# Decode rows of a Mamba-2 mixer turned into columns by four TensorE transposes instead of four fp32 matmuls on identity columns

## The chip, the cores and the metric

One NeuronCore of a Trainium2 chip runs the whole kernel. The metric is the device time of one execution in microseconds (us); lower is better. The kernel works on five engines, each with its own instruction stream: TensorE (PE in the profile, with PEld for its weight loads), VectorE (DVE), ScalarE (ACT), GpSimd (POOL) and SyncE (SP), which issues most DMAs. They meet only through semaphores.

## The reference, cut to what matters

The program is one inference step of a two-layer decoder for two request groups that share the weights: a prompt of 256 tokens and eight decode sequences of one token each (so 264 columns in all). Layer 0 has a Mamba-2 mixer. What the change touches is the decode side of its state-space step, which for one token is

```python
def step(h, inp):                      # T = 1 for the decode sequences
    s_c, dec_c = inp                   # dt * x * B^T, exp(dt * a)
    return h * dec_c[..., None, None] + s_c, h
...
y_inter = jnp.einsum('bclgn,bcgepn->bclgep', cc, h_in) * jnp.exp(cum)[..., None]
y = (y_intra + y_inter)
```

With one token that is y = exp(dt a) (C . h0) + dt (C . B) x. There are 8 groups g, each with 4 heads of 64 values (256 rows of output per sequence) and a state width of 128.

## The kernel before, in words

Everything is kept with channels on the 128 partitions and the 264 tokens along the free axis. Weights come in units of 1024 columns into a ring of four buffers; ScalarE rounds a unit to its high part (`whi`, L985), VectorE computes the rest (`wlo`, L1407), and TensorE makes three products for each tile (L436, L437, L438), 24 products for a unit of the mixer's input projection.

The mixer's input projection ("sin") has 49 units. Its loop runs over slots `s_`, on every engine in the same order: slot `s_` starts with unit `s_`, and other work is put between units by tables: `CHUNK_AT = [14, 17, 21, 25, 30, 35, 41, 46]` (the prompt's scan, two chunks of 128 tokens for each group: `chunk_in(2g)` in that slot, `chunk_in(2g+1)` and `chunk_out(2g)` one later, `chunk_out(2g+1)` two later), `DEC_AT = [16, 19, 23, 27, 32, 37, 43, 46]` (the decode rows) and `NORM_AT`. The order is written out by hand; no planner moves anything. VectorE takes the finished unit out of its bank (`take`, L1454) at the start of its own slot and lags TensorE by up to some microseconds; the semaphores decide by how much.

The decode path of a group g runs so:

- `decode_rows(g)`, TensorE, slot `DEC_AT[g]` (L799): eight matmuls whose stationary operand is C of one sequence, broadcast over 32 columns, put C . h0 into bank 7: 128 rows by 512, where 32 rows in a row hold the same numbers (sequence q mod 4 by row, q div 4 by half of the bank).
- `copy_rows(g)`, ScalarE, same slot (L1188): bank 7 into `crow` in SBUF.
- `decode_columns(g)`, TensorE, slot `DEC_AT[g] + 1` (L814, L816): the 256 rows are wanted as channels on partitions. Four fp32 matmuls with a 128x128 slice of `crow` as stationary operand and four columns of the identity (`ident[:, 0:P:32]`) as moving operand write 16 columns into bank 2; a fifth matmul with `ones` adds the sum over the state of B C, 8 columns. An fp32 matmul appears in the profile as two passes, so L814 has 8 records for each group.
- `decode_read(g)`, VectorE, slot `DEC_AT[g] + 2`, after `take` (L1718, L1720): two small products out of bank 2. GpSimd adds the parts up (L2068, L2069).

Bank 7 is used for one more thing: the differences of the odd chunks, written by `chunk_in(2g+1)` (`diff = bank[5 + 2 * c]`, L759 and L760) and read by ScalarE's `decay_exp(2g+1)` (L1181). Its users before wait on `dec_copied` (the copy to `crow` is done) and on `ssd_exp` (the exponential is done).

Of the kernel before, what the change touches and what calls it, by code (L numbers as in the profile page):

```python
# [19 lines left out]
ALU = mybir.AluOpType  # L20
AX = mybir.AxisListType

P = 128
# [3 lines left out]
SEQS = 8  # L27
N = T + SEQS
# [4 lines left out]
G = 8  # L33
# [61 lines left out]
CHUNK_AT = [14, 17, 21, 25, 30, 35, 41, 46]  # L95
# [3 lines left out]
DEC_AT = [16, 19, 23, 27, 32, 37, 43, 46]  # L99
# [17 lines left out]
def h0_turn(g):  # L117

    return H0_BUF[:g + 1].count(H0_BUF[g])
# [30 lines left out]
def trunk_kernel(nc, weights, xT, pT, cst, vec, convst, ssm0, kcT, vc_in, ck, cv,  # L150
# [3 lines left out]
    with ExitStack() as ctx:  # L154
        def sb(name, shape, dt=F32):
            return ctx.enter_context(nc.sbuf_tensor(name, shape, dt))

        def sem(name):
            return ctx.enter_context(nc.semaphore(name))
# [9 lines left out]
        with nc.sbuf_tensor("under", [P, 2 * FT * N], F32) as under:  # L169
# [4 lines left out]
            crow = under[:, 40 * N + 256:40 * N + 768]  # L174
# [20 lines left out]
        bank = [ctx.enter_context(nc.psum_tensor(f"bank{b}", [P, 512], F32)) for b in range(4)]  # L195
# [5 lines left out]
        ident, tri, ones = cs[:, C_ID:C_ID + P], cs[:, C_TRI:C_TRI + P], cs[:, C_ONE:C_ONE + P]  # L201
# [49 lines left out]
        dec_copied = sem("dec_copied")  # L251
        dec_sel = sem("dec_sel")
        dec_read = sem("dec_read")
# [10 lines left out]
        ssd_exp = sem("ssd_exp")  # L264
# [78 lines left out]
        da_d = sb("da_d", [P, XT, SEQS])  # L343
        dt_d = sb("dt_d", [P, XT, SEQS])
        dtx_d = sb("dtx_d", [P, G, SEQS, 2])
        bc_d = sb("bc_d", [P, G, SEQS])
# [26 lines left out]
        w1 = [guf[:, 576 + 16 * b:592 + 16 * b].rearrange("p (k s) -> p k s", k=2) for b in range(2)]  # L373
        w2 = [guf[:, 608 + 16 * b:624 + 16 * b].rearrange("p (k s) -> p k s", k=2) for b in range(2)]
# [55 lines left out]
        def _(pe):  # L430
            pe.sem_inc(unit_used, RING)

            def split_products(out, w, tile, rh, rl, start, stop):

                c = slice(tile * P, tile * P + P)
                pe.matmul(out, whi[:, w, c], rh, start=start, stop=False)  # L436
                pe.matmul(out, whi[:, w, c], rl, start=False, stop=False)  # L437
                return pe.matmul(out, wlo[:, w, c], rh, start=False, stop=stop)  # L438
# [233 lines left out]
            def sout_part(j, tiles, last=False):  # L672

                pe.wait_ge(lo_ready, U0["sout"] + j + 1)
                pe.wait_ge(hl_ready, HREADY["sout"] + j + 1)
                for m in tiles:
                    mm = split_products(bank[m][:, 0:N], (U0["sout"] + j) % RING, m, hh[:, j, :], hl[:, j, :], j == 0, False)
                if last:
                    mm.then_inc(unit_used, 1)
# [59 lines left out]
            def chunk_in(k):  # L739

                g, c = k // 2, k % 2
                r = slice(128 * c, 128 * c + 128)
                if c == 0:
                    pe.wait_ge(conv_act, 4 * g + 4)
                if k > 0:
                    pe.wait_ge(ssd_read, k)
                pe.matmul(bank[4][:, 0:128], xact[:, 16 + g, r], xact[:, 24 + g, r], start=True, stop=True)
                pe.transpose(bank[4][:, 128:256], xact[:, 16 + g, r], ident)
                pe.transpose(bank[4][:, 256:384], xact[:, 2 * g, r], ident)
                pe.transpose(bank[4][:, 384:512], xact[:, 2 * g + 1, r], ident).then_inc(ssd_in, 1)  # L750
                pe.wait_ge(ssd_sel, k + 1)
                if k > 1:
                    pe.wait_ge(ssd_exp, k - 1)
                if c == 1:
                    pe.wait_ge(dec_copied, [d_ < CHUNK_AT[g] + 1 for d_ in DEC_AT].count(True))
                if k == 0:
                    pe.wait_ge(pre_const, 1)
                diff = bank[5 + 2 * c][:, 0:512]
                pe.matmul(diff, diffLg[k % 2], diffR[c], start=True, stop=False)  # L759
                pe.matmul(diff, ident_r, mask_r.unsqueeze(1).to_broadcast([P, 4, P]), start=False, stop=True).then_inc(ssd_diff, 1)  # L760
# [22 lines left out]
            def add_inter(g):  # L783

                pe.wait_ge(ssd_isc, g + 1)
                for n_ in range(2):
                    mm = pe.matmul(bank[6][:, 256 * n_ + 128:256 * n_ + 256], isc[:, 128 * n_:128 * n_ + 128], ident,
                                   start=False, stop=True, skip_group_check=True)
                mm.then_inc(ssd_tr, 1)

            def decode_rows(g):

                pe.wait_ge(h0_landed[H0_BUF[g]], 16 * h0_turn(g))
                pe.wait_ge(dec_act, g + 1)
                pe.wait_ge(ssd_exp, 2 * [c_ + 1 < DEC_AT[g] for c_ in CHUNK_AT].count(True))
                if g > 0:
                    pe.wait_ge(dec_copied, g)
                for q in range(SEQS):
                    mm = pe.matmul(bank[7][32 * (q % 4):32 * (q % 4) + 32, 256 * (q // 4):256 * (q // 4) + 256],  # L799
                                   dact[:, g, 1, q:q + 1].to_broadcast([P, 32]), h0buf[H0_BUF[g]][:, 256 * q:256 * q + 256], start=True, stop=True)  # L800
                mm.then_inc(h0_used, 1)

            def decode_columns(g):

                pe.wait_ge(dec_copied, g + 1)
                pe.wait_ge(dec_prod, g + 1)
                if g > 0:
                    pe.wait_ge(dec_read, g)
                if DEC_AT[g] + 1 > NORM_AT[3]:
                    pe.wait_ge(gated_std, 1)  # L810
                c_ = N + 24 * g
                for i in range(2):
                    for t in range(2):
                        pe.matmul(bank[2][:, c_ + 8 * t + 4 * i:c_ + 8 * t + 4 * i + 4], crow[:, 256 * i + 128 * t:256 * i + 128 * t + 128],  # L814
                                  ident[:, 0:P:32], start=True, stop=True)
                pe.matmul(bank[2][:, c_ + 16:c_ + 24], ones, bc_d[:, g, :], start=True, stop=True).then_inc(dec_sel, 1)  # L816

            def norm_sums(g):

# [54 lines left out]
            for s_ in range(len(SIN)):  # L874
                if s_ == 1:
                    unit_pair("sin", 0)
                elif s_ > 1:
                    sin_unit(s_)
                if s_ == PRE_AT:
                    pre_tokens()  # L880
                if s_ == PRE_AT + 3:
                    pre_sums()
                for g in range(G):
                    if s_ == CHUNK_AT[g] + 3:
                        add_inter(g)
                if s_ in DEC_AT:
                    decode_rows(DEC_AT.index(s_))
                for g in range(G):
                    if s_ == CHUNK_AT[g]:
                        chunk_in(2 * g)  # L890
                    if s_ == CHUNK_AT[g] + 1:
                        chunk_in(2 * g + 1)
                        chunk_out(2 * g)
                    if s_ == CHUNK_AT[g] + 2:
                        chunk_out(2 * g + 1)
                if s_ in NORM_AT:
                    norm_sums(NORM_AT.index(s_))
                if s_ - 1 in DEC_AT:
                    decode_columns(DEC_AT.index(s_ - 1))
            pe.wait_ge(ssd_read, 2 * G)  # L900
            pe.wait_ge(ssd_exp, 2 * G)
            sout_part(0, (4, 5, 7))
            add_inter(G - 1)
            pe.wait_ge(a_free, A0["f2i0"] + 4)
# [496 lines left out]
        def _(dve):  # L1401
# [308 lines left out]
            def decode_read(g):  # L1710

                dve.wait_ge(dec_sel, g + 1)
                if g == 0:
                    dve.wait_ge(pre_a, 3)
                if g >= 2:
                    dve.wait_ge(dec_y, g - 1)
                c_ = N + 24 * g
                dve.tensor_tensor(w1[g % 2], bank[2][:, c_ + 16:c_ + 24].unsqueeze(1).to_broadcast([P, 2, SEQS]),  # L1718
                                  dtx_d[:, g].rearrange("p s t -> p t s"), ALU.mult)
                dve.tensor_tensor(w2[g % 2], bank[2][:, c_:c_ + 16].rearrange("p (k s) -> p k s", k=2), da_d[:, 2 * g:2 * g + 2, :], ALU.mult).then_inc(dec_read, 1)  # L1720

            def by_head(a):
                return a.rearrange("p (h w) -> p h w", h=4)
# [66 lines left out]
            for s_ in range(SLOTS):  # L1790
                kind, i = SIN[s_] if s_ < len(SIN) else ("", 0)
# [9 lines left out]
                if s_ - 2 in DEC_AT:  # L1801
                    decode_read(DEC_AT.index(s_ - 2))
# [537 lines left out]
```

## Time and profile before

| | before |
|---|---|
| median of 3 runs | 1229.14 us (1228.28 to 1231.04) |
| profiled execution, first to last instruction (span) | 1227.6 us |
| TensorE busy | 1202.2 us, 98% |
| VectorE, ScalarE, GpSimd busy | 882.4, 686.4, 232.8 us |
| chain that ended last, share by engine | PE 69%, DVE 16%, ACT 7%, issue 6%, DMA 2% |
| granted TensorE clock, mean | 0.994 |

For the profiled execution only the span is given, no total of its own; the median of the runs shown is 1.5 us above it. A busy TensorE is not a TensorE at its peak: the matmuls are pipelined, a record of 0.28 us follows the one before it after 0.12 us. The distance between starts is therefore what an instruction costs TensorE.

### The profile page before, as it was taken

What the parts mean: (1) busy time and instruction counts of PE and PEld (TensorE: products, weight loads), DVE (VectorE), ACT (ScalarE), POOL (GpSimd) and SP (SyncE); (2) the same over time, 40 slices, a digit from 0 to 9 for tenths busy, and PEclk for the clock granted to TensorE, in tenths of its full rate; (3) what the DMA queues carried; (4) which work ended last, traced back from release to release, by engine and by line L of the source; (5) the groups of instructions that cost most, each with busy time, mean ns of one, the idle gap of its engine ahead of it and who ended that gap; (6) DMA issues with size and microseconds to landing.
All of it is one profiled execution on the core that took longest, in us unless ns stands there. A gap on an engine that the chain in (4) does not pass through costs nothing.

```text
span 1227.6 us, 26707 instructions
## 1 busy us (share of the span) xinstructions
PE 1202.2 (98%) x9875; PEld 1169.6 (95%) x9875; DVE 882.4 (72%) x1405; ACT 686.4 (56%) x1096; POOL 232.8 (19%) x338
## 2 busy tenths in 40 slices
PE   6999999999999999999999999999999999999998
PEld 6999999898988899999999899999998899999998
DVE  5666646998888867786745987787379657767448
ACT  6454435676576556556546765555357555454345
POOL 0100002312221201232344323232024310000001
PEclk9999999999999999999999999999999899999999
DMA  7655544654453445867786577656642235555552
GB/s 270 235 202 184 186 174 142 246 188 155 160 166 122 164 157 203 319 214 260 265 300 234 176 286 276 220 187 233 235 142 87 79 121 207 186 180 179 180 180 88
DMA packets 61424, 239.08 MB, mean 195 GB/s; under 512 B 7080, under 2 KB 8272, under 8 KB 56976
## 3 DMA queue, kind: packets, MB, share of 16 engines
q1 hardware_dynamic: 55008, 197.01, 45.5%
q0 software_dynamic: 6064, 40.66, 9.2%
q8 instruction: 42, 0.69, 0.2%
q10 hardware_dynamic: 288, 0.54, 0.1%
q14 instruction: 22, 0.18, 0.0%
HBM read 226.87 MB, written 13.39 MB: 196 GB/s over the span
## 4 chain that ended last, share of the span: by engine, by line
PE 69%; DVE 16%; ACT 7%; issue 6%; DMA 2%; DVEq 0%; SPq 0%; ACTq 0%
PE bank L436 21%; PE bank L437 21%; PE bank L438 21%; DVE wlo L1407 5%; ACT whi L985 3%; DVE xact L1662 1%; DVE gu L1466 1%; DVE xl L1426 1%; DMA raw<-weights 1%; DVE gu L1454 1%; DVE x L1437 1%; ACT L1181 1%; DMA x<-xT 1%; DMA xact<-stat_rows 1%; ACT under L1324 0%
## 5 line engine op out<-in xcount | busy, mean ns | idle before, releaser
L1407 DVE TENSOR_TENSOR wlo<-raw,whi 128x1024 fp32r<-128x1024 f32 x369 | 462.5, 1257 | 253.5 <-ACT whi L985 251.4
L436 PE MATMUL bank<-xh,whi 128*128 128x264 f32 x2024 | 582.1, 288 | 13.9 <-DVE xl L1426 11.7
L437 PE MATMUL bank<-xl,whi 128*128 128x264 f32 x2024 | 575.0, 284 | 0.0
L438 PE MATMUL bank<-xh,wlo 128*128 128x264 f32 x2024 | 574.5, 284 | 0.0
L985 ACT ACTIVATE whi<-raw 128x1024 fp32r<-128x1024 f32 x369 | 387.5, 1054 | 249.5 <-PE bank L438 228.3
L436 PEld LDWEIGHTS bank<-xh,whi 128*128 128x128 f32 x2024 | 382.6, 189 | 18.0 <-issue 11.6
L437 PEld LDWEIGHTS bank<-xl,whi 128*128 128x128 f32 x2024 | 382.8, 189 | 0.9
L438 PEld LDWEIGHTS bank<-xh,wlo 128*128 128x128 f32 x2024 | 380.9, 188 | 0.0
L436 PE MATMUL bank<-hh,whi 128*128 (+1 forms) x896 | 255.8, 286 | 1.1 <-ACT zs L1310 0.5
L438 PE MATMUL bank<-hh,wlo 128*128 (+1 forms) x896 | 255.1, 285 | 0.0
L437 PE MATMUL bank<-hl,whi 128*128 (+1 forms) x896 | 254.4, 284 | 0.0
L436 PEld LDWEIGHTS bank<-hh,whi 128*128 128x128 f32 x896 | 168.6, 188 | 2.8 <-issue 1.3
L437 PEld LDWEIGHTS bank<-hl,whi 128*128 128x128 f32 x896 | 169.1, 189 | 0.1
L438 PEld LDWEIGHTS bank<-hh,wlo 128*128 128x128 f32 x896 | 168.6, 188 | 0.0
L1052 ACT ACTIVATE hh<-gu 128x264 fp32r<-128x264 f32 (+1 forms) x88 | 37.4, 425 | 167.8 <-DVE gu L1466 167.8
L2008 POOL TENSOR_TENSOR sq<-sq 128x264 f32<-128x264 f32 x49 | 39.1, 798 | 459.2 <-ACT sq L1023 453.9
L1454 DVE TENSOR_TENSOR gu<-bank,rstd 128x264 f32<-128x264 f32 x192 | 82.0, 429 | 16.5 <-PE bank L438 15.1
L1471 DVE TENSOR_TENSOR hl<-gu,hh 128x264 f32 (+1 forms) x88 | 42.4, 482 | 28.7 <-ACT hh L1052 28.7
L2144 POOL TENSOR_TENSOR xact<-xact,da_bc 128x512 f32<-128x512 f32 x32 | 38.7, 1211 | 100.6 <-PE bank L438 100.6
L1662 DVE SCALAR_TENSOR_TENSOR xact<-under,vs,xact 128x256 f32<-128x256 f32 x96 | 46.6, 485 | 2.3
L1466 DVE TENSOR_TENSOR gu<-gu 128x264 f32<-128x264 f32 x88 | 44.2, 502 | 0.2 <-ACT gu L1047 0.2
L2149 POOL TENSOR_TENSOR xact<-xact 128x512 f32<-128x512 f32 x20 | 31.0, 1550 | 57.5 <-PE bank L438 57.5
(309 smaller groups left out, 1000.7 us busy)
## 6 DMA issues: line engine op xcount, KB each, us to landing
raw<-weights SPq DMA_DIRECT2D x369, 512.0 KB, 3.5
under<-ssm POOLq DMA_DIRECT2D x8, 1024.0 KB, 7.4
xact<-ssm POOLq DMA_DIRECT2D x8, 1024.0 KB, 7.7
out_ssm_s<-xact POOLq DMA_DIRECT2D x8, 1024.0 KB, 5.4
xact<-dtx_rows POOLq DMA_DIRECT2D x5, 1024.0 KB, 10.8
zs<-dtx_rows POOLq DMA_DIRECT2D x2, 1024.0 KB, 14.6
x<-xT SPq DMA_DIRECT2D x2, 528.0 KB, 6.9
xact<-stat_rows POOLq DMA_DIRECT2D x2, 528.0 KB, 6.2
```

The lines of the kernel that those rows point to most:

```text
L436: pe.matmul(out, whi[:, w, c], rh, start=start, stop=False)
L437: pe.matmul(out, whi[:, w, c], rl, start=False, stop=False)
L438: return pe.matmul(out, wlo[:, w, c], rh, start=False, stop=stop)
L985: act.activation(whi[:, s, :], raw[:, s, :], ACT.Copy).then_inc(hi_ready, 1)
L1052: act.activation(dst, gu[:, 2 * p + 1, :], ACT.Copy).then_inc(hh_ready, 1)
L1407: dve.tensor_tensor(wlo[:, s, :], raw[:, s, :], whi[:, s, :].bitcast(F32), ALU.subtract).then_inc(lo_ready, 1)
L1454: dve.tensor_tensor(dst, src[:, 0:N], rstd[:, :], ALU.mult).then_inc(a_free, 1)
L1466: dve.tensor_tensor(gu[:, 2 * p + 1, :], gu[:, 2 * p, :], gu[:, 2 * p + 1, :], ALU.mult).then_inc(h_ready, 1)
L1471: dve.tensor_tensor(one(hl), gu[:, 2 * p + 1, :], one(hh).bitcast(F32), ALU.subtract).then_inc(hl_ready, 1)
L1662: dve.scalar_tensor_tensor(out=out, in0=xr[:, k:k + T], scalar=vs[:, V_CW + CT * k + c:V_CW + CT * k + c + 1], in1=out, op0=ALU.mult, op1= ...
L2008: pool.tensor_tensor(sq3[:, 0, :], sq3[:, 0, :], sq3[:, m, :], ALU.add).then_inc(sq_pair, 1)
L2144: pool.tensor_tensor(by_head(part), by_head(part), da_bc[:, 2 * k:2 * k + 2, 4 * q:4 * q + 4].unsqueeze(3).to_broadcast([P, 2, 4, 64]), AL ...
```

## The change

The four matmuls on identity columns become four full transposes of 128x128, which write all 512 columns of bank 7, over the rows they came from. VectorE then reads every 32nd column of bank 7 (16 of them) and keeps the 8 columns of the sum in bank 2. The waits change with it: whoever writes bank 7 next has to wait for VectorE's read (`dec_read`) and no longer only for ScalarE's copy, and the transposes have to wait until ScalarE has read the differences that lie in bank 7.

```
 chunk_in(k), odd chunks:
                 if c == 1:
                     pe.wait_ge(dec_copied, [d_ < CHUNK_AT[g] + 1 for d_ in DEC_AT].count(True))
+                    pe.wait_ge(dec_read, [d_ < CHUNK_AT[g] for d_ in DEC_AT].count(True))
 decode_rows(g):
                 if g > 0:
-                    pe.wait_ge(dec_copied, g)
+                    pe.wait_ge(dec_read, g)
 decode_columns(g):
                 pe.wait_ge(dec_copied, g + 1)
                 pe.wait_ge(dec_prod, g + 1)
-                if g > 0:
-                    pe.wait_ge(dec_read, g)
                 if DEC_AT[g] + 1 > NORM_AT[3]:
                     pe.wait_ge(gated_std, 1)
-                c_ = N + 24 * g
-                for i in range(2):
-                    for t in range(2):
-                        pe.matmul(bank[2][:, c_ + 8 * t + 4 * i:c_ + 8 * t + 4 * i + 4], crow[:, 256 * i + 128 * t:256 * i + 128 * t + 128],
-                                  ident[:, 0:P:32], start=True, stop=True)
-                pe.matmul(bank[2][:, c_ + 16:c_ + 24], ones, bc_d[:, g, :], start=True, stop=True).then_inc(dec_sel, 1)
+                pe.wait_ge(ssd_exp, 2 * [c_ <= DEC_AT[g] for c_ in CHUNK_AT].count(True))
+                for n_ in range(4):
+                    pe.transpose(bank[7][:, P * n_:P * n_ + P], crow[:, P * n_:P * n_ + P], ident)
+                pe.matmul(bank[2][:, N + 8 * g:N + 8 * g + 8], ones, bc_d[:, g, :], start=True, stop=True).then_inc(dec_sel, 1)
 after the last slot, ahead of the first products of the output projection (banks 4, 5, 7):
+            pe.wait_ge(dec_read, G)
 decode_read(g), VectorE:
-                dve.tensor_tensor(w2[g % 2], bank[2][:, c_:c_ + 16].rearrange("p (k s) -> p k s", k=2), da_d[:, 2 * g:2 * g + 2, :], ALU.mult).then_inc(dec_read, 1)
+                dve.tensor_tensor(by_half(w2[g % 2]), bank[7][:, 0:512:32].rearrange("p (i k q) -> p k i q", i=2, k=2), by_half(da_d[:, 2 * g:2 * g + 2, :]),
+                                  ALU.mult).then_inc(dec_read, 1)
```

(`by_half` is a view that splits the last axis of 8 into 2 by 4; the first product of `decode_read` only reads from other columns of bank 2.)

## Rows read from the trace of the kernel before

**Rows 1.** Window, length, busy us of PE, PEld, DVE, ACT, POOL, clock, DMA, GB/s.

```profile
250.00:300.00 50.00, 49.36 (x411) 44.72 (x410) 44.06 (x89) 34.02 (x57) 11.23 (x31) 1.00 0.49 178
```

**Rows 2.** The chain that ended last: start us, us, what. Pieces within the mixer.

```profile
273.12 0.79 PE bank L814 x8
...
288.85 0.99 PE bank L814 x8
...
376.84 0.79 PE bank L814 x8
...
401.11 1.22 DVE wlo L1407
...
456.02 0.39 PE bank L436
```

**Rows 3.** PE, slot 17: start us, us, line, op, out<-in, shape.

```profile
272.17 0.27 PE L748 MATMUL bank<-cs,xact 128*128 128x128 f32 x1
272.28 0.27 PE L749 MATMUL bank<-cs,xact 128*128 128x128 f32 x1
...
272.96 0.95 PE L814 MATMUL bank<-cs,under 128*128 128x4 f32 x8
273.77 0.37 PE L816 MATMUL bank<-bc_d,cs 128*128 128x8 f32 x2
...
274.33 0.28 PE L438 MATMUL bank<-xh,wlo 128*128 128x264 f32 x1
274.45 0.28 PE L436 MATMUL bank<-xh,whi 128*128 128x264 f32 x1
```

**Rows 4.** One line's instructions (L746, a further wait ahead of L747): ns min/median/max.

```profile
L746 PEldq EVENT_SEMAPHORE  x7: 51/51/51, 270.6 to 409.1; - x7
```

**Rows 5.** Slot 18, chunk 3: TensorE's differences, then VectorE's take and decode read.

```profile
277.46 0.48 PE L759 MATMUL bank<-hl 128*128 128x512 f32 x1
...
278.64 0.42 DVE L1454 TENSOR_TENSOR under<-bank,rstd 128x264 f32<-128x264 f32 x1
...
279.06 0.16 DVE L1720 TENSOR_TENSOR gu<-bank,da_d 128x16 f32<-128x16 f32 x1
```

**Rows 6.** The same pair in slot 22, then read 6 and the rows of group 7.

```profile
293.62 0.16 DVE L1720 TENSOR_TENSOR gu<-bank,da_d 128x16 f32<-128x16 f32 x1
...
407.52 0.16 DVE L1720 TENSOR_TENSOR gu<-bank,da_d 128x16 f32<-128x16 f32 x1
...
297.31 0.48 PE L759 MATMUL bank<-hl 128*128 128x512 f32 x1
...
409.11 1.07 PE L799 MATMUL bank<-under,dact 128*32 128x256 f32 x16
```

**Rows 7.** Slots 47 and 48: TensorE, ScalarE's exponential of chunk 15, VectorE's read 7.

```profile
417.04 1.06 PE L814 MATMUL bank<-cs,under 128*128 128x4 f32 x8
417.95 0.37 PE L816 MATMUL bank<-bc_d,cs 128*128 128x8 f32 x2
418.17 0.37 PE L436 MATMUL bank<-xh,whi 128*128 128x264 f32 x1
...
418.46 0.58 ACT L1181 ACTIVATE sq<-bank 128x512 f32<-128x512 f32 x1
...
422.32 0.17 DVE L1720 TENSOR_TENSOR gu<-bank,da_d 128x16 f32<-128x16 f32 x1
```

**Rows 8.** Windows with TensorE waits; columns as in Rows 1.

```profile
236.00:240.00 4.00, 3.04 (x25) 3.07 (x25) 3.93 (x8) 2.71 (x4) 1.89 (x4) 1.00 0.58 180
700.00:704.00 4.00, 2.13 (x11) 1.92 (x12) 3.58 (x7) 2.56 (x6) 2.38 (x3) 0.79 0.01 4
```

**Rows 9.** PE in the second of these windows, by start us.

```profile
700.67 0.39 PE L436 MATMUL bank<-xh,whi 128*128 128x264 f32 x1 [0.98 <-DVE xl L1426]
...
702.87 0.59 PE L436 MATMUL bank<-xh,whi 128*128 128x264 f32 x1 [1.21 <-DVE xl L1426]
...
705.67 0.33 PE L436 MATMUL bank<-xh,whi 128*128 128x264 f32 x1
```

More of the change, by code:

```diff
@@ L1716, in decode_read @@
                     dve.wait_ge(dec_y, g - 1)
-                c_ = N + 24 * g
-                dve.tensor_tensor(w1[g % 2], bank[2][:, c_ + 16:c_ + 24].unsqueeze(1).to_broadcast([P, 2, SEQS]),
+                by_half = lambda a: a.rearrange("p k (i q) -> p k i q", i=2)
+                dve.tensor_tensor(w1[g % 2], bank[2][:, N + 8 * g:N + 8 * g + 8].unsqueeze(1).to_broadcast([P, 2, SEQS]),
                                   dtx_d[:, g].rearrange("p s t -> p t s"), ALU.mult)
-                dve.tensor_tensor(w2[g % 2], bank[2][:, c_:c_ + 16].rearrange("p (k s) -> p k s", k=2), da_d[:, 2 * g:2 * g + 2, :], ALU.mult).then_inc(dec_read, 1)
+                dve.tensor_tensor(by_half(w2[g % 2]), bank[7][:, 0:512:32].rearrange("p (i k q) -> p k i q", i=2, k=2), by_half(da_d[:, 2 * g:2 * g + 2, :]),
+                                  ALU.mult).then_inc(dec_read, 1)
             def by_head(a):
```

## The prediction

> **What bounds the kernel now.** I read the busy times by window first. Between 250 and 300 us TensorE is busy for 49.4 of 50 us and VectorE for 44.1 [rows 1]: nobody has room there, and a gain on one engine can stop at the other. So the second view is the chain that ended last. In the mixer it changes sides. The old column matmuls (L814) lie on it for groups 0, 1, 2, 3 and 5, in pieces of 0.79, 0.99, 0.79, 0.79 and 0.79 us (the first two and the last of the five stand in [rows 2]): there TensorE sets the pace, and what it saves is saved. For groups 4, 6 and 7 the chain runs over VectorE and ScalarE (one of its pieces is the `wlo` at 401.11), and this stretch lasts from about 392 us until TensorE takes over again at 456.02 [rows 2]; a TensorE saving in it is worth nothing. The third view is the order in time on TensorE, VectorE and ScalarE around the two places where the change adds a wait.
>
> **The saving.** A transpose of this very shape is in the kernel: L748 and L749 start 0.11 us apart [rows 3]. Four of them are 0.44 us. The old columns cost 0.81 us from their start to the start of L816 in slot 17 [rows 3], 0.79 us as a piece of the chain, 0.99 for group 1 [rows 2], and 0.91 us for group 7 [rows 7]. The fifth matmul stays. So a group saves 0.35 us, group 1 0.55, group 7 0.47. If all five groups on the chain kept it: 4 x 0.35 + 0.55 = 1.95 us.
>
> The record of a transpose lasts 0.27 us, although the next one starts after 0.11 [rows 3]. The Trainium skill ("TensorE: Matmul & The Clock Gate", Part 4: PE-mode transpose) gives about 275 ns for a 128x128 transpose inside a kernel, and says that transposes do not count towards the full clock like matmuls do. The record agrees with the 275 ns; the distance between two of them does not, and it is the distance that TensorE pays. With 0.27 us each the change would lose on its own account, which is a rival below.
>
> **VectorE's read.** The second product (L1720) reads 16 elements in either form; it takes 0.16 us [rows 5]. A take of 264 elements out of a bank is 0.42 us [rows 5], so the stride can cost between 0 and 0.26 us for each group. With 16 elements I take 0, the row that is the nearest; at the other end, 8 reads would be 2.1 us.
>
> **More waits in TensorE's queue.** Each odd chunk waits on one semaphore more. A wait that needs an instruction of its own is 0.051 us in TensorE's sequencer [rows 4]. Seven odd chunks: between 0 and 0.36 us; I take 0, since the sequencer runs ahead of the array wherever TensorE is busy. `decode_columns` swaps one wait for another.
>
> **The first new wait that is late: chunk 3, slot 18.** The differences of an odd chunk now need `dec_read` of every decode group whose columns were written before. For chunk 3 that is read 0. TensorE starts these differences (L759) at 277.46. VectorE's read 0 (L1720) starts at 279.06 and ends at 279.22, right behind the take of unit 18 at 278.64 [rows 5]; VectorE was busy or waiting for ScalarE before it, not for TensorE, so it comes no earlier when TensorE does. TensorE restarts about 0.1 us after the read, at 279.3: 1.85 us later than before, and the 0.35 us saved by group 0 disappears in the same wait. Queued behind it are the two difference matmuls, `chunk_out(2)` and unit 19; for these wait ScalarE (rounding the next unit into the ring), and VectorE's takes. From there TensorE is on the chain until 298, so nothing absorbs it: +1.85 us.
>
> For the other odd chunks the read is one slot earlier. In slot 22 read 1 starts at 293.62 and the differences at 297.31 [rows 6], a margin of 3.5 us; chunks 7 to 15 are the same or wider. `decode_rows` now waits for the read of the group before; the closest is group 7, read 6 ending at 407.68 against 409.11 [rows 6], 1.4 us of margin. These waits cost nothing.
>
> **The second one: columns of group 7, slot 47.** The transposes go into bank 7, so they need the exponential of the last odd chunk issued. For groups 0 to 6 `decode_rows` has waited for that already (the counts are equal). For group 7, chunk 15 comes between rows and columns in the same slot. TensorE reaches the columns at 417.04; ScalarE runs the exponential of chunk 15 from 418.46 to 419.04 [rows 7]. So TensorE stands still for 2.0 us, plus 0.15 for the release. Behind it is unit 48, the last of the projection (418.17 before [rows 7]), then `chunk_out(15)`, for which VectorE's carry, the gate, the last group's norm and its round trip through DRAM wait, all on the chain. The exponential itself hangs on VectorE and ScalarE, so this wait moves with them and is not eaten up by an earlier one. 2.15 - 0.47 (group 7's saving) = +1.7 us.
>
> The wait added at the end of the loop is for read 7, which ended at 422.49 [rows 7]. It follows the take of unit 48; TensorE has `chunk_out(15)`, 1.4 us, to do after unit 48. It costs nothing.
>
> **The sum.** First wait +1.85; savings of groups 1, 2, 3, 5 behind it 0.55 + 3 x 0.35 = -1.6; second wait +1.7. Together +1.95 us at the end of the mixer. After it TensorE has no idle time into which this could vanish until the chain is on it again at 456.02 [rows 2].
>
> **The clock.** Between 700 and 704 us TensorE was busy for 2.13 of 4 us, with waits of 0.98 and 1.21 us, and the mean granted clock was 0.79 [rows 8, 9]: it had dropped from 2.4 to 1.2 GHz, and twelve products from 702.87 to 705.67 took 2.80 us [rows 9] instead of 12 x 0.12 = 1.44, the distance in rows 3. That is 1.3 us, of which I count 1.2, since the first product always starts slowly. Between 236 and 240, with 3.04 of 4 us busy and a wait of 1.29 us at the beginning, the clock stayed at 1.00 [rows 8]. The two new waits are of 2.0 to 2.2 us in one piece, nearer to the first case, and the second lies among small matmuls. I take it that the clock falls after one of the two: +1.2 us. The bounds are 0 and 2.4.
>
> 1.95 + 1.2 = +3.15 us. The profiled span would go from 1227.6 to 1230.8 us, and the median of the runs, 1.5 us above the span, from 1229.14 to about 1232.3.
>
> **The rivals.**
>
> A. *Two waits, no drop of the clock*: +1.95, 1231.1 us. For it: the clock stood through 1.29 us of waiting. Against: the two waits are of 2.0 us and more in one piece, where 2.19 us in two pieces went with a drop [rows 9].
>
> B. *The saving is the whole effect, faster*: the two waits are met. It takes a read 0 that ends before 277.1 us and an exponential of chunk 15 that ends before 417.0, that is VectorE 2.1 us and ScalarE 2.0 us earlier; from that point the change gains 1.95 us, 1227.2 us. For it: the trace is of one execution, and others may have VectorE nearer to TensorE. Against: both margins are missed by 2 us, in a stretch where VectorE is full.
>
> C. *Only one wait costs*, because the ring of weights filled while TensorE stood or because the second is absorbed before the carry: with the first alone 1.85 - 1.6 = +0.25, with the second alone 1.7 - 1.95 = -0.25: 1229 to 1229.4 us, no change.
>
> D. *A transpose costs its record*, 0.27 us: a group then pays 1.09 instead of 0.79, +0.3, where the sum had -0.35. On the five groups that count (1, 2, 3, 5, 7) that is 1.5 us lost instead of 2.07 gained: 1.95 + 3.55 = +5.5, 1234.6 us, more with the clock. The rule of the Trainium skill above would give this. Against it stand the sixteen transposes of each kind in the prompt's chunks, of which rows 3 show two.
>
> **How the numbers follow.** Waits and one or two drops of the clock 0.45; A 0.32; B 0.08; C 0.11; D 0.04. The forecast is the likeliest, 1232.3; A lies at 1231.1 and two drops at 1233.5. The range 1229.7 to 1233.8 holds the forecast's case, A, and part of C, and leaves out B and D and a read that costs its upper bound. What a measurement can tell from no change is 0.2%, 2.46 us: slower means above 1231.6. Slower: nearly all of the forecast's case, a third of A, and D, 0.57. Faster (under 1226.7) a part of B: 0.06. Same: 0.37.
>
> **What the profile after would show.** L814 would be gone and four transposes 0.11 us apart in its place, eight times. TensorE would have two idle stretches with names: L759 in slot 18, 1.9 to 2.2 us, ended by VectorE's decode read, and the first transpose of group 7, about 2.0 us, ended by ScalarE's exponential. Unit 22 and later should start earlier relative to unit 20 than before by 0.35 to 0.55 us. The clock would be under 1.00 in a window behind one of the waits. It would be wrong if read 0 came earlier than TensorE, if the spacing of the transposes were above 0.2 us, or if the differences of another odd chunk waited.

## The result, and the profile after

| | before | after |
|---|---|---|
| median of 20 runs each | 1228.26 us (1223.92 to 1231.04) | 1231.73 us (1227.26 to 1234.28) |
| ratio after to before, 95% interval | | 1.0028 (1.002 to 1.0036) |
| span of the profiled execution | 1227.6 us | 1232.1 us |
| TensorE busy | 1202.2 us | 1202.2 us |
| granted TensorE clock, mean of the profiled execution | 0.994 | 0.993 |

The change makes the kernel 0.28% slower, +3.5 us by the medians (forecast: +3.15). The forecast time of 1232.3 us was counted from the median of 3 runs, 1229.14; the median of 20 is 0.9 us lower. So the time came out 0.6 us under the forecast and the difference 0.35 us over it. The profiled execution of the changed kernel is the slowest of its 20 (1234.28 us), so what it shows is on the dear side. TensorE's busy time is the same to the tenth although it has less to do; the busy time cannot show the loss. The list of TensorE's waits does (line, what ended them, us in total, times, longest us). These are the four longest in the mixer of the changed kernel, 225 to 465 us:

```profile
PE bank L812 <- ACT sq L1179: 2.2, 1, 2.2
PE bank L760 <- DVE gu L1718: 2.1, 1, 2.1
PE bank L436 <- DVE under L1452: 1.3, 1, 1.3
PE bank L747 <- ACT xact L1151: 1.2, 1, 1.2
```

The first two are new and are the two that the prediction named: the transposes of group 7 behind ScalarE's exponential, and the differences of chunk 3 behind VectorE's decode read. Line numbers have moved by a few: L760 is the old L759, L1718 the old L1720, L812 are the transposes, L813 the old L816. The third wait was there before, with 1.29 us. The fourth was there with 0.69 us; what it has grown by is what group 4 saves ahead of it (see e11 below).

Slot 17 in order of time, changed kernel, against [rows 3] (start us, us, engine, line, op):

```profile
271.35 0.60 PE L812 MATMUL bank<-cs,under 128*128 128x128 f32 x4
271.79 0.29 PE L813 MATMUL bank<-bc_d,cs 128*128 128x8 f32 x2
271.93 0.37 PE L436 MATMUL bank<-xh,whi 128*128 128x264 f32 x1
```

The four transposes take 0.44 us to the start of L813, where the columns took 0.81; L813 itself costs 0.14 instead of 0.23 us. The first new wait, with the two engines side by side, against [rows 5]:

```profile
277.77 0.47 PE L760 MATMUL bank<-hl 128*128 128x512 f32 x1 [2.14 <-DVE gu L1718]
...
277.03 0.42 DVE L1452 TENSOR_TENSOR under<-bank,rstd 128x264 f32<-128x264 f32 x1
277.38 0.16 DVE L1716 TENSOR_TENSOR gu<-bank,dtx_d 128x16 f32<-128x16 f32 x1
277.46 0.16 DVE L1718 TENSOR_TENSOR gu<-bank,da_d 128x16 f32<-128x16 f32 x1
```

The read out of bank 7 with a stride of 32 takes 0.16 us, as before, and ends at 277.62; TensorE restarts at 277.77. Of TensorE's wait of 2.14 us, 0.46 us is group 0's saving, which brings TensorE to it earlier; behind the old columns, in e4, the same wait is 1.68 us. The second wait, against [rows 7]:

```profile
417.49 1.09 PE L812 MATMUL bank<-cs,under 128*128 128x128 f32 x4 [2.24 <-ACT sq L1179]
418.37 0.43 PE L813 MATMUL bank<-bc_d,cs 128*128 128x8 f32 x2
418.65 0.57 PE L436 MATMUL bank<-xh,whi 128*128 128x264 f32 x1
419.02 0.42 PE L437 MATMUL bank<-xl,whi 128*128 128x264 f32 x1
419.24 0.42 PE L438 MATMUL bank<-xh,wlo 128*128 128x264 f32 x1
...
424.10 0.66 PE L774 MATMUL bank<-sq 128*64 128x128 f32 x8
```

```profile
416.77 0.58 ACT L1179 ACTIVATE sq<-bank 128x512 f32<-128x512 f32 x1
```

Here is the third part of the loss. These four transposes take 0.88 us instead of 0.44, the products of unit 48 start 0.22 us apart instead of 0.12, and the unit takes 5.45 us (418.65 to 424.10). The windows show the clock (columns as in rows 1, granted clock behind the five engines):

```profile
274.00:278.00 4.00, 1.86 (x15) 1.65 (x15) 3.09 (x8) 2.73 (x4) 0.48 (x2) 1.00 0.64 240
414.00:418.00 4.00, 1.76 (x9) 0.96 (x8) 3.76 (x9) 2.49 (x4) 0.00 (x0) 0.88 0.36 124
418.00:424.00 6.00, 6.00 (x29) 5.96 (x27) 2.28 (x5) 1.49 (x3) 0.00 (x0) 0.51 0.28 92
```

Behind the second wait the clock was at 1.2 GHz until 424 us; behind the first, of nearly the same length, it stayed at 2.4 GHz in this execution (1.00 from 270 to 290 us).

**A ruler.** Executions start up to 1.6 us apart in the profile's time, so I measure from one matmul ahead of everything the change touches, the 64x64 one of L849, to three waits that every kernel has: M1, the first L773 that waits for VectorE (slot 22); M2, the second one (slot 42); M3, the product of the output projection that takes the chain over from VectorE. In the kernel before, M3 starts at 456.02 [rows 2], the other three at

```profile
232.23 0.27 PE L849 MATMUL bank<-cs,small 64*128 64x64 f32 x1 [0.52 <-ACT small L1201]
298.66 0.66 PE L773 MATMUL bank<-sq 128*64 128x128 f32 x8 [0.64 <-DVE sq L1758]
392.08 0.66 PE L773 MATMUL bank<-sq 128*64 128x128 f32 x8 [0.45 <-DVE sq L1758]
```

and all four in the changed kernel at

```profile
230.64 0.27 PE L846 MATMUL bank<-cs,small 64*128 64x64 f32 x1 [0.54 <-ACT small L1199]
298.43 0.66 PE L774 MATMUL bank<-sq 128*64 128x128 f32 x8 [0.62 <-DVE sq L1757]
390.46 0.66 PE L774 MATMUL bank<-sq 128*64 128x128 f32 x8 [0.45 <-DVE sq L1757]
458.62 0.38 PE L436 MATMUL bank<-hh,whi 128*128 x1 [0.37 <-DVE wlo L1405]
```

So M1 is 67.79 us from the ruler's zero against 66.43, M2 159.82 against 159.85, M3 227.98 against 223.79. The first wait less group 1's saving is +1.36, the savings of groups 2, 3 and 5 between M1 and M2 give it all back (-1.39), and the last stretch costs +4.22. What lies behind M3 is not used: it takes 768.2 to 773.5 us in the twelve profiles, although its code is the same in all. In the changed kernel's profile it is 773.5, 1.9 us more than in that of before, so the two spans differ by 4.5 us though the mixer accounts for +4.19 and the stretch ahead of the ruler's zero for -1.6.

### The profile page after: what moved, and what is told of

The parts are those of the page before. It is cut to its first block, busy times and chain, and to the rows that moved or that the text cites. A ratio compares the mean times of both kernels' runs of the same rounds, so it can differ in the third digit from the quotient of the medians.

```text
span 1232.1 us, 26650 instructions
## 1 busy us (share of the span) xinstructions
PE 1202.2 (98%) x9843; PEld 1167.7 (95%) x9843; DVE 885.5 (72%) x1405; ACT 686.8 (56%) x1096; POOL 229.6 (19%) x338
## 4 chain that ended last, share of the span: by engine, by line
PE 72%; DVE 16%; ACT 6%; issue 4%; DMA 2%; DVEq 0%; SPq 0%; ACTq 0%
PE bank L436 23%; PE bank L437 22%; PE bank L438 22%; DVE wlo L1405 5%; ACT whi L983 2%; DVE xact L1660 2%; DVE xl L1424 1%; DMA raw<-weights 1%; ACT L1179 1%; DVE under L1452 1%; DVE x L1435 1%; DVE gu L1452 1%; DVE rstd L1446 1%; DMA xact<-stat_rows 1%; DVE gu L1464 0%
## 5 line engine op out<-in xcount | busy, mean ns | idle before, releaser
L1469 DVE TENSOR_TENSOR hl<-gu,hh 128x264 f32 (+1 forms) x88 | 47.2, 536 | 28.7 <-ACT hh L1050 28.7
L1424 DVE SCALAR_TENSOR_TENSOR xl<-x,vs,xh 128x264 fp32r<-128x264 f32 x64 | 39.0, 621 | 2.3 <-ACT xh L1018 2.1
```

The costliest lines, as they stand in the source:

```text
L1424: dve.scalar_tensor_tensor(out=xl[:, m, :], in0=x[:, m, :], scalar=vs[:, gain + m:gain + m + 1], in1=xh[:, m, :].bitcast(F32), op0=ALU.mul ...
L1469: dve.tensor_tensor(one(hl), gu[:, 2 * p + 1, :], one(hh).bitcast(F32), ALU.subtract).then_inc(hl_ready, 1)
```

## The experiments

Each kernel was run 11 or 12 times (e4 6 times) beside the kernel before; the intervals are at 95%. "Mixer" is M3 of its profile less the 223.79 of before. "Clock loss" is (1 - mean granted clock) x span, averaged over the runs of a kernel; the kernel before has 4.9 to 5.4 us of it in its three samples (29, 35 and 23 runs). It counts every stretch at 1.2 GHz, not those in the mixer alone: all twelve profiles have one between 950 and 990 us, and those of before, e1, e2 and e8 another at 700 to 710. It also counts low clock in which TensorE stands idle and loses nothing, so it is an upper bound of what the clock costs: among the 87 runs of the kernel before, a run with 1 us more of it is 0.6 to 0.7 us longer.

| kernel | ratio to before (95%) | medians, this and before, us | M1 | M2-M1 | M3-M2 | mixer | clock loss, us |
|---|---|---|---|---|---|---|---|
| before | 1 | | 66.43 | 93.42 | 63.94 | 0 | 4.9 to 5.4 |
| after | 1.0028 (1.002 to 1.0036) | 1231.73, 1228.26 | 67.79 | 92.03 | 68.16 | +4.19 | 7.6 |
| e1: group 0 old | 1.0013 (1.0002 to 1.0024) | 1227.97, 1227.36 | 65.91 | 92.05 | 65.50 | -0.33 | 7.3 |
| e2: group 7 old | 1.0016 (1.0005 to 1.0028) | 1229.90, 1227.36 | 69.39 | 92.03 | 63.94 | +1.57 | 7.8 |
| e3: groups 0, 7 old | 0.9995 (0.9982 to 1.0008) | 1226.14, 1227.36 | 65.91 | 92.04 | 63.91 | -1.93 | 5.8 |
| e4: waits alone | 1.0053 (1.0037 to 1.0069) | 1233.37, 1227.36 | 68.33 | 93.42 | 67.34 | +5.30 | 7.6 |
| e6: wait 2 alone | 1.0029 (1.0019 to 1.0039) | 1231.32, 1227.70 | 66.43 | 93.45 | 67.72 | +3.81 | 7.8 |
| e10: filled waits | 1.0005 (0.9991 to 1.0018) | 1227.95, 1227.70 | 67.91 | 92.03 | 65.47 | +1.62 | 4.2 |
| e8: read 0 early | 0.9996 (0.9983 to 1.0008) | 1228.22, 1227.70 | 65.58 | 92.05 | 66.78 | +0.62 | 6.5 |
| e9: both mended | 0.999 (0.9977 to 1.0004) | 1226.29, 1227.70 | 65.60 | 92.02 | 63.97 | -2.20 | 5.5 |
| e12: e9 again | 0.999 (0.9978 to 1.0001) | 1225.70, 1228.16 | 65.58 | 92.06 | 64.01 | -2.14 | 5.8 |
| e11: e9, 4 and 6 old | 0.9996 (0.9984 to 1.0007) | 1226.35, 1228.16 | 65.60 | 92.05 | 63.98 | -2.16 | 5.9 |

**Undoing the change for one group.** In e1, e2 and e3 the groups of `OLD_FORM` keep the old columns, and the differences of the odd chunks do not wait for the reads of such groups on their account; `decode_rows(g)` keeps its wait for the read of the group before. (Only `decode_columns` is shown.)

```
 decode_columns(g):
+    if g in OLD_FORM:                       # (0,), (7,), (0, 7)
+        for i in range(2):
+            for t in range(2):
+                c_ = N + 64 + 16 * g + 8 * t + 4 * i
+                pe.matmul(bank[2][:, c_:c_ + 4], crow[:, 256 * i + 128 * t:256 * i + 128 * t + 128], ident[:, 0:P:32], ...)
+    else:
         pe.wait_ge(ssd_exp, ...)
         for n_ in range(4): pe.transpose(...)
```

Group 0 old. 

> Group 0 alone keeps the old four column matmuls (written to free columns of bank 2); groups 1 to 7 have the transposes, so the differences of chunk 3 wait for no read. Theory (the loss is in two late waits, the second with a drop of the clock): TensorE's idle of 2.1 us ahead of L760 in slot 18 is gone, group 0 pays its 0.35 us again, so about 1.8 us less than the changed kernel, about +1.5 us against before (1229.8 at 1228.3 for before). The wait for ScalarE's exponential ahead of group 7's transposes and the low clock behind it stay. Rival (the transposes, or VectorE's read with a stride out of bank 7, cost more than what they replace): one group of eight less, 0.4 us less than the changed kernel, +3.0 against before.

Group 7 old. 

> Group 7 alone keeps the old column matmuls, groups 0 to 6 have the transposes. Theory: the wait for the exponential of chunk 15 is gone, and with it the low clock from there to the end of unit 48; what is left is the first wait (+1.85) less the savings behind it (-1.6): 0 to +0.3 us against before, so the same time as before. If the clock cost nothing and the wait alone went away: 1.7 us less than the changed kernel, +1.7 against before. Rival (transposes or strided read dear): +3.0 against before.

Groups 0 and 7 old. 

> Groups 0 and 7 keep the old column matmuls, groups 1 to 6 have the transposes: both late waits are gone, the saving stays. Theory: groups 1, 2, 3 and 5 on the chain save 0.55 + 3 x 0.35 = 1.6 us: 1.6 us under before, ratio 0.9987; no TensorE idle over 1.3 us after the start, clock 1.00 from 20 to 900 us. Rival: at least +2 us against before, since six of eight groups still have the transposes and the read out of bank 7.

Measured: +1.6 us by the ratio for e1 (expected +1.5), +2.0 for e2 (expected 0 to +0.3, or +1.7 if the clock cost nothing), -0.6 for e3 with an interval of -2.2 to +1.0 (expected -1.6). TensorE's waits in e1:

```profile
230.70 0.27 PE L858 MATMUL bank<-cs,small 64*128 64x64 f32 x1 [0.52 <-ACT small L1211]
296.61 0.66 PE L779 MATMUL bank<-sq 128*64 128x128 f32 x8 [0.63 <-DVE sq L1773]
388.66 0.66 PE L779 MATMUL bank<-sq 128*64 128x128 f32 x8 [0.45 <-DVE sq L1773]
415.76 0.63 PE L824 MATMUL bank<-cs,under 128*128 128x128 f32 x4 [2.24 <-ACT sq L1191]
...
454.16 0.38 PE L439 MATMUL bank<-hh,whi 128*128 x1 [0.28 <-DVE wlo L1417]
```

The first wait is gone with one group's transposes, the second is there with 2.24 us, and in this execution the clock did not fall behind it: the transposes record 0.63 us, not 1.09, and M2 to M3 is 65.50. That is the bare price of the second wait, less group 7's saving behind it: 65.50 - 63.94 = +1.56 us. The mixer of this one profile is 0.33 us shorter than before, and the ratio over the runs is +1.6 us all the same; their mean clock loss of 7.3 us, 2.4 more than that of the kernel before beside them, says that in other executions the clock does fall. In e2 it is the other way round:

```profile
279.14 0.47 PE L765 MATMUL bank<-hl 128*128 128x512 f32 x1 [2.14 <-DVE gu L1734]
301.39 0.66 PE L779 MATMUL bank<-sq 128*64 128x128 f32 x8 [0.63 <-DVE sq L1773]
```

```profile
279.00:284.00 5.00, 4.86 (x26) 4.24 (x27) 4.51 (x9) 3.06 (x5) 1.93 (x6) 0.67 0.39 131
```

M2 to M3 is 63.94 us, to the hundredth what it was before the change; but the clock fell behind the first wait (0.67 from 279 to 284 us), and M1 is 1.6 us later than in the changed kernel, where it had not. That is where most of e2's missing 2 us are: the expectation had given the first wait no drop of the clock. Either wait can be followed by a drop. Of the three profiles with the first wait (changed kernel, e2, e4) one has it behind that wait; of the five with the second (changed kernel, e1, e4, e6, e8) four have it behind that one. The program alone does not fix it: the mean clock of the changed kernel's 20 runs lies between 0.992 and 0.997. The rival (dear transposes, a dear read) falls with e3: six of eight groups have both, and its mixer is 1.93 us shorter than before; in the time +2 us lies outside its interval.

**The waits without the transposes.** e4 adds both waits to the kernel before and changes nothing else, e6 only the second.

```
 chunk_in(k), odd chunks (e4 alone):
+    pe.wait_ge(dec_read, [d_ < CHUNK_AT[g] for d_ in DEC_AT].count(True))
 decode_columns(g) (e4 and e6), ahead of the four matmuls:
+    pe.wait_ge(ssd_exp, 2 * [c_ <= DEC_AT[g] for c_ in CHUNK_AT].count(True))
```

Both waits. 

> The kernel before, with the old column matmuls and the old reads, and only two waits added: odd chunks for the decode reads, the columns for the exponentials. Nothing that the waits protect is there. Theory: both idle stretches appear, 1.85 and 2.1 us, and no saving stands against them: +4 us against before, and with the clock as low behind the second as in the changed kernel +5.2 to +6.5. Rival (the cost lies in the transposes or the strided read): no change against before, 0 +- 0.3 us.

The second alone. 

> The kernel before with one wait added, the columns' wait for the exponentials; nothing else of the change. Theory: one idle stretch of 2.1 us ahead of group 7's columns: mixer +2.0 us at full clock and +3.4 where the clock falls behind it, nothing before it; in the time +2.0 to +3.4. Rival (this wait is absorbed by the chain over VectorE and ScalarE that sets the end there): 0 to +0.5.

Measured +6.5 us (4.5 to 8.5) for e4 and +3.6 us (2.3 to 4.8) for e6, the first at the upper end of what was expected, the second just above it. The waits in e4:

```profile
278.54 0.47 PE L760 MATMUL bank<-hl 128*128 128x512 f32 x1 [1.68 <-DVE gu L1722]
...
420.27 1.03 PE L816 MATMUL bank<-cs,under 128*128 128x4 f32 x8 [2.07 <-ACT sq L1183]
```

M1 is 1.90 us late and M2 - M1 is 93.42, unchanged: the first wait costs 1.9 us, and the same wait in the odd chunks between M1 and M2 costs nothing that 0.01 us would show, nor does its instruction. A kernel with no transpose in it is slower than the changed one (1.0053 against 1.0028). Between M1 and M2, where no clock fell in either, it is slower by 1.39 us, which is what the transposes of groups 2, 3 and 5 save.

**Keeping TensorE at work while it waits.** e10 is the changed kernel with 22 matmuls of 184 columns ahead of each of the two waits; their results are never read. (Ahead of the first it also waits for the exponential of chunk 2, which has left the bank they write.)

```
+    for _ in range(22):
+        pe.matmul(bank[5][:, 0:184], xh[:, 0, 0:P], xh[:, 0, 0:184], start=True, stop=True)   # chunk 3; bank[2][:, 328:512] for group 7
     pe.wait_ge(...)
```

> The changed kernel with 22 single-pass matmuls of 184 columns (results never read) ahead of each of the two late waits, about 2 us of work where TensorE stood idle; the waits themselves are unchanged. Theory (part of the loss is the clock behind the waits): the clock stays at 1.00 in the whole mixer, in this and every run, and what is left is the bare waiting: mixer +1.5 us against before, +1.5 in the time as well, that is 2 us less than the changed kernel. Rival (the clock is noise, and the median loss is all in the waits and elsewhere): +3.4 as the changed kernel.

Measured: +0.6 us (-1.1 to +2.2) against before. The fillers and what follows:

```profile
415.73 2.70 PE L818 MATMUL bank<-xh 128*128 128x184 f32 x22
418.27 0.60 PE L821 MATMUL bank<-cs,under 128*128 128x128 f32 x4
...
418.85 0.37 PE L438 MATMUL bank<-xh,whi 128*128 128x264 f32 x1
419.06 0.29 PE L439 MATMUL bank<-xl,whi 128*128 128x264 f32 x1
```

```profile
410.00:430.00 20.00, 19.41 (x150) 16.75 (x149) 15.75 (x34) 11.67 (x21) 3.13 (x5) 1.00 0.35 109
```

The waits cost what they cost before, and a little more (the fillers take 2.54 us where the wait would have taken 2.1 to 2.24): mixer +1.62. But the clock stays up behind both, and the mean clock loss over 12 runs is 4.2 us, against 7.6 in the changed kernel. Useless work makes this kernel 2.8 us faster than the changed one by the ratios (1.0005 against 1.0028, each to its own runs of before). Not all of that need be the clock behind the two waits: 4.2 us is also less than the 5.4 that the kernel before had beside it, and no run says why. So the clock is shown to have a share in the loss, and 2.8 us is more likely too much for it than too little.

**Mending it.** e8 moves VectorE's read of group 0 one slot earlier, ahead of chunk 2; e9 does this and leaves group 7 in the old form; e12 is e9 once more; e11 has groups 4 and 6 in the old form too.

```
 VectorE, in slot order:
-    if s_ - 2 in DEC_AT:
+    if s_ - 2 in DEC_AT and s_ - 2 != DEC_AT[0]:
         decode_read(DEC_AT.index(s_ - 2))
     if last == "conv":
         conv_taps(li)
+    if s_ - 1 == DEC_AT[0]:
+        decode_read(0)
```

Read 0 early. 

> The changed kernel with VectorE's decode read of group 0 moved from behind the take of slot 18 to slot 17, behind the taps and ahead of chunk 2; all eight groups keep the transposes. Theory: read 0 is done some 2 us before TensorE comes to the differences of chunk 3, the first idle stretch is gone and group 0 keeps its 0.35 us: mixer up to the second wait 2.3 us under before, the second wait stays (+1.56), so -0.7 us with the clock up and +0.6 to +1.9 where it falls behind the second wait. Rival (the first wait cost nothing in the end, what is lost there is won back from VectorE): as the changed kernel, +3.4.

Both. 

> Both mended at once: read 0 in slot 17, and group 7 with the old column matmuls, so neither wait is late. Theory: 0.5 + 0.35 us before the first milestone, 1.4 behind it: mixer 2.3 us shorter than before, ratio 0.998, no TensorE idle over 1.3 us in it, clock 1.00. Rival: no better than before, since VectorE has to wait for the columns of group 0 and hands this on.

Both, second sample. 

> The same kernel as e9 (read 0 in slot 17, group 7 with the old column matmuls), a second sample on another chip allocation, because the interval of the first, 0.9977 to 1.0004, does not exclude no change. Theory: mixer 2.2 us shorter than before again, ratio 0.998. Rival (the gain is given back behind the mixer): 1.000.

Fewer transposes. 

> As e12, but groups 4 and 6 keep the old column matmuls too, so transposes are left only in groups 0, 1, 2, 3 and 5, those whose columns lay on the chain that ended last. Theory (a TensorE saving in groups 4 and 6 is worth nothing, VectorE sets the end there): the mixer ends where that of e12 does, within 0.1 us, and TensorE's wait for VectorE near group 4 is 0.46 us shorter (0.7 instead of 1.2). Rival (every transpose counts, wherever it is): 0.9 us later than e12.

Measured: e8 -0.5 us (-2.1 to +1.0), e9 -1.2 (-2.8 to +0.5), e12 -1.2 (-2.7 to +0.1), e11 -0.5 (-2.0 to +0.9). For e8 -0.7 to +1.9 was expected; the rival's +3.4 is outside its interval. For e9 and e12 0.998 was expected; their intervals hold 0.998 as well as 1, so the times do not decide between the theory and its rival. The same goes for e11 against e12. The mixers are sharper: e8's is +0.62, with a drop of the clock behind the second wait, where -0.7 at full clock and +0.6 to +1.9 with a drop was expected. e12 and e11, at the wait near group 4 and at M3, with their zeros at 231.54 and 231.41:

```profile
358.17 0.49 PE L750 MATMUL bank<-xact 128*128 128x128 f32 x2 [1.16 <-ACT xact L1163]
...
453.19 0.39 PE L439 MATMUL bank<-hh,whi 128*128 x1 [0.31 <-DVE wlo L1417]
```

```profile
358.06 0.49 PE L750 MATMUL bank<-xact 128*128 128x128 f32 x2 [0.70 <-ACT xact L1163]
...
453.04 0.38 PE L439 MATMUL bank<-hh,whi 128*128 x1 [0.31 <-DVE wlo L1417]
```

M3 is 221.65 and 221.63 us from the zero: what the transposes of groups 4 and 6 save goes into TensorE's wait (1.16 against 0.70), as expected. The version with both waits mended beats the changed kernel clearly (0.999 against 1.0028). That it beats the kernel before is shown for the mixer, -2.20 and -2.14 us in two profiles, and not for the whole time: both intervals reach past 1.

## Why the prediction was right, point by point

- *Which groups' savings count.* Right. Group 1 shortens M1 by 0.52 us (e1, e3), groups 2, 3 and 5 shorten M2 - M1, groups 4 and 6 shorten nothing (e11), group 0's saving is lost in the first wait, and group 7's lies behind the second.
- *The saving.* The transposes: 0.81 to 0.44 us, as forecast. That "the fifth matmul stays" was wrong in size: behind the transposes it costs 0.14 us instead of 0.23. So a group saves 0.46 us and not 0.35, and M2 - M1 fell by 1.39 us, where 3 x 0.35 = 1.05 was counted. I had counted the distance from the first column matmul to the fifth matmul, and taken the distance from there to the next product as fixed. For group 1 the 0.99 us of the chain was too much: by the distance between starts it went from 0.92 to 0.49 us, and its whole saving of 0.52 is under the 0.55 counted.
- *VectorE's read and TensorE's further waits at zero.* Right: 0.16 us for the read in either form; M2 - M1 of e4 equal to that of before to 0.01 us.
- *The first wait, +1.85.* Measured +1.90 (M1 of e4). Less group 1's saving of 0.52 it left +1.36.
- *The second wait, +1.7 after group 7's saving.* Measured +1.56 at full clock (e1).
- *The margins of the other waits.* Right: no third new wait appears in the list of TensorE's waits.
- *The sum without the clock, +1.95.* By the profiles 1.36 - 1.39 + 1.56 = +1.53; e10's mixer, with its longer fillers, +1.62. The forecast was 0.4 us too high: 0.3 through the savings (1.91 instead of 1.6), 0.1 through the second wait.
- *The clock, +1.2.* The mechanism was right, its size was too small. What one drop costs varies: 1.28 us in e8 (M3 - M2 of 66.78 against 65.50), 1.60 in e2 (M1 of 69.39 against 67.79), and 2.66 in the changed kernel (68.16 - 65.50), since it stayed down from before 417.49 to 424 us, longer than in [rows 9]. Over all runs the clock loss rose from about 5.1 to 7.6 us, +2.5, the upper bound. With the 0.6 to 0.7 us of span for each us of it, an estimate is +1.6.
- *The sum, +3.15; measured +3.5 (2.5 to 4.4).* The terms as measured give 1.53 + 1.6 to 2.5 = 3.1 to 4.0. The two errors of size, 0.4 too much without the clock and 0.4 to 1.3 too little with it, have opposite signs. That the sum is nearer than its terms is in part luck.

Of the rivals, A (no drop of the clock) is refuted as the common case: the clock loss is 7.6 us instead of 5.1, and 13 of the 20 runs have a mean clock under 0.994, which none of the 87 runs of the kernel before has. Single executions go A's way at one wait or the other. B (the waits are met) did not happen in this kernel; e9 does away with both waits by other means, an earlier read 0 and the old columns for group 7, and gets -2.2 us in the mixer, where B had 1.95 with the smaller saving. C (one wait is absorbed) is refuted by e6, where the second alone costs 3.6 us, and by e2, where the first alone is left: +2.0 us with the savings, where C had +0.25. D (a transpose costs its record of 0.27 us) is refuted by the 0.44 us for four; the 275 ns of the Trainium skill ("TensorE: Matmul & The Clock Gate", Part 4) agree with the record and not with what a transpose costs TensorE. Whether transposes count less for the clock, as that part says, no run here separated: e10 keeps the clock up with ordinary matmuls ahead of them.

## What to carry to other kernels

A result that is put back into a buffer saves the buffer but lengthens its occupation to the next reader, and each waiter for it has to be checked against the trace: which instruction of which engine frees it, when it does, and who stands behind the waiter. Here sixteen such waits were added or tightened (seven odd chunks behind a decode read, seven times `decode_rows`, the columns of group 7, the end of the loop). Two were late, each by about 2 us, and these two with the clock outweighed eight savings of about 0.46 us, of which three, those of groups 0, 4 and 6, had nowhere to go. Where a new wait of TensorE is as long as these (1.7 to 2.2 us in one piece), count a drop of the clock behind it as a likely part of the price, 1.3 to 2.7 us when it came here, and where the order can be changed, move the read that frees the buffer ahead of the bulk work on its engine, as e9 does.

## What the runs showed of the hardware that was not expected

- A matmul on a stationary `ones` with 8 moving columns cost 0.22 to 0.23 us (from its start to the next product's) behind fp32 matmuls on 4 columns and 0.14 to 0.15 us behind transposes, in all groups at full clock, and in e11, which has both forms, too. In these places a matmul's cost goes with what stands ahead of it; why is open.
- The length of the low clock varies. Behind a wait of 2.24 us it was at 1.2 GHz for unit 48 as a whole (5.45 us), in another kernel's execution it did not fall behind the same wait (e1), in a third it fell behind the other wait (e2). In e6 it fell late: TensorE restarted at 417.82 us, its products were 0.12 us apart until 420.2, and then 0.22. One profile is no measure of it; the mean clock of every run is a better one.
- 22 matmuls whose results nobody reads, put at each of the two places where TensorE stood idle, go with a clock loss of 4.2 us over 12 runs, against 7.6 in the changed kernel and 5.4 in the kernel before beside it.
